# First token tile ahead of the second around the first expert gather: cross output, norm, queries and first list in another order

## The chip, the cores and the metric

The kernel runs on one core of one Trainium2 chip. The metric is the device time of one execution in microseconds; lower is better. The core has TensorE (PE, matmuls), VectorE (DVE), ScalarE (ACT), GpSimd (POOL) and SyncE (SP), which run their own instruction streams and meet at semaphores, and 16 DMA engines that move data for all of them.

## The reference

Batch 1, 256 tokens (two token tiles of 128), width 1024, float32. A first block (mLSTM, attention, gated feed-forward) is followed by a second block with two layers. Each layer has a mixer, a cross attention to 256 memory rows, and an expert layer that picks 128 of 16384 experts for each token (8 heads, 16 each):

```python
for l in range(2):
    h = h + mixer_l(rmsnorm(h, mix_norm[l]))
    h = h + memory_cross_attn(rmsnorm(h, xattn_norm[l]), mem_n, wq[l], wkv[l], wo[l])
    h = h + peer_ffn(rmsnorm(h, peer_norm[l]), peer_wq[l], peer_keys[l], peer_u[l], peer_v[l])

# peer_ffn, per token:
q = (xb @ wq).reshape(T, 8, 2, 128)
s = einsum('thpd,hpnd->thpn', q, sub_keys)                 # 2 x 128 scores per head
s1, i1 = top_k(s[:, :, 0], 16);  s2, i2 = top_k(s[:, :, 1], 16)
cand = s1[..., :, None] + s2[..., None, :]                 # 256 candidates per head
top, pos = top_k(cand, 16)                                 # and with pos the expert numbers eid
act = gelu(einsum('td,ted->te', xb, u[eid]))
y = einsum('te,ted->td', softmax(top) * act, v[eid])
```

## The kernel before

Everything is one program, written out by hand for each engine; the order of the instructions is the order of the code. Weights lie in HBM as tiles of 128 x 4096 float32 (2 MB), cut into four parts of 512 KB (0.524 MB). SP loads the parts in one fixed order (`tiles_in_order`, `weights_in_order`) into a ring of 6 parts (`W`, `RAW_RING`): a part is asked for when the part six places before it has been used. A tile can serve both token tiles; in `product` it does so part by part. In `one_tile` one token tile uses the whole weight tile, and its parts are given back only in the pass with `last` true.

PSUM has 8 banks. `Plan` deals them out in the order of `add`: each stage claims the next bank and waits until ScalarE or VectorE (its taker) has emptied the stage before it there.

The expert layer is four chains, (layer, token tile) = (0,0), (0,1), (1,0), (1,1), of 128 rows each. A row j is one gather by POOL (L789): for each of the 128 tokens the row of u and v of its j-th expert, 1.05 MB. Eight slots (`rows_a`, `rows_b`, `rows_c`) form a ring; slot n is refilled when TensorE has used row n-8 (`rows_done`). Two rows are a group: VectorE takes their dot products with the token (`dots`, L2511), ScalarE makes weights and two diagonal matrices of them (L1621 to L1632), TensorE adds v by them to the sum (`weigh`, L953, 4 matmuls of 512 columns in a group). `lead(c)` begins a chain and `feed()` does one group, and these calls are strewn among the other work of each engine, so that gathers run beside everything from the first one on. `drain()` does what is left of a chain.

The expert numbers come from VectorE in portions of two heads (32 rows): `top_lists` (the 16 best of 128 scores, four lists), `top_heads` (candidates, the 16 best of 256, twice), `top_keys` (from positions to expert numbers `p_eid`), `top_gates` (softmax over ScalarE's `top_exp`). The first portion stands ahead of the first row. The others are hung into the groups of chain 0 by the table `LISTS_AT[0]` (group: which chain and pair of heads), candidates 3 groups and key numbers 5 groups behind a list. POOL waits for `eid_ready` at every 32nd row.

The change lies in `joint`, the stage from the cross attention of layer 0 to the weights of layer 1's memory keys and values, where both token tiles are worked on together. In it stand, in this order on TensorE: query tiles `x_q`, scores `x_s`, transposes `x_t`, values `x_pv`, turned heads `x_oT`, output `x_o` (both weight tiles, token tile 0 then 1 for each), the turned normed tiles `T6.0` and `T6.1`, the expert queries and scores `p_q0` to `p_q3` and `p_s0` to `p_s3`, and the key and value tiles of layer 1, `x_k1` and `x_v1`, with the first groups of chain 0 among them.

## Time and profile before

| | us |
|---|---|
| median of 3 runs | 2315.01 |
| lowest, highest | 2313.47, 2315.64 |
| the profiled execution | 2322.3 |
| its span, first to last instruction | 2320.5 |

| engine | busy us | share of the span |
|---|---|---|
| PE | 2026.2 | 87% |
| DVE | 1498.7 | 65% |
| POOL | 926.9 | 40% |
| ACT | 766.8 | 33% |

777.34 MB are moved in all, 559.83 MB of them by POOL's queue, at a mean of 335 GB/s. The chain that ended last is 46% PE, 25% DMA and 21% DVE. A busy share is an average over stages with different limits; what a change in one stage is worth is read from the waits in that stage. Times in the trace count from the span's start. A float32 matmul leaves two records on PE, so x64 there stands for 32 matmuls.

### The profile page before, as it was taken

What the parts mean: (1) busy time and instruction counts of PE and PEld (TensorE: products, weight loads), DVE (VectorE), ACT (ScalarE), POOL (GpSimd) and SP (SyncE); (2) the same over time, 40 slices, a digit from 0 to 9 for tenths busy, and PEclk for the clock granted to TensorE, in tenths of its full rate; (3) what the DMA queues carried; (4) which work ended last, traced back from release to release, by engine and by line L of the source; (5) the groups of instructions that cost most, each with busy time, mean ns of one, the idle gap of its engine ahead of it and who ended that gap; (6) DMA issues with size and microseconds to landing.
All of it is one profiled execution on the core that took longest, in us unless ns stands there. A gap on an engine that the chain in (4) does not pass through costs nothing.

```text
span 2320.5 us, 25004 instructions
## 1 busy us (share of the span) xinstructions
PE 2026.2 (87%) x8348; PEld 1264.2 (54%) x8348; DVE 1498.7 (65%) x3776; ACT 766.8 (33%) x1771; POOL 926.9 (40%) x688
## 2 busy tenths in 40 slices
PE   8999999999999899997779988869999978777776
PEld 4855589878776455442345554624665536232322
DVE  5777523143324778886777776868786677877755
ACT  2323144444131333332333333233424222333332
POOL 2721368766421333443333233243323232444442
PEclk9999999999999999999999999999999989999999
DMA  8556455555324999999999999999999999999997
GB/s 321 213 192 211 173 182 191 196 199 198 138 100 159 423 423 422 419 391 420 423 420 398 391 419 420 418 421 385 423 379 389 377 420 369 399 416 425 413 425 298
DMA packets 139761, 777.34 MB, mean 335 GB/s; under 512 B 15512, under 2 KB 17688, under 8 KB 73072
## 3 DMA queue, kind: packets, MB, share of 16 engines
q0 software_dynamic: 79248, 559.83, 58.9%
q1 hardware_dynamic: 60240, 215.86, 25.0%
q8 instruction: 66, 1.08, 0.2%
q14 instruction: 63, 0.52, 0.1%
q10 hardware_dynamic: 144, 0.05, 0.0%
HBM read 774.62 MB, written 1.06 MB: 334 GB/s over the span
## 4 chain that ended last, share of the span: by engine, by line
PE 46%; DMA 25%; DVE 21%; ACT 4%; issue 2%; POOL 1%; SPq 0%; DVEq 0%; ACTq 0%; POOLq 0%
PE banks L953 14%; PE banks L842 14%; DMA rows_c<-in_uv,p_eid 12%; PE banks L990 7%; DMA W<-in_weights 6%; DMA rows_b<-in_uv,p_eid 5%; PE banks L1199 2%; DVE rows_b L2511 2%; DVE rows_c L2511 2%; DVE arena L2024 2%; DVE arena L2511 2%; DMA arena<-in_uv,p_eid 2%; PE banks L1429 2%; ACT arena L1623 1%; DVE arena L2280 1%
## 5 line engine op out<-in xcount | busy, mean ns | idle before, releaser
L953 PE MATMUL banks<-arena 128*128 128x512 f32 x712 | 348.1, 626 | 93.1 <-ACT arena L1632 92.8
L789 POOL DMA_INDIRECT arena<-in_uv,p_eid x192 | 219.3, 1142 | 495.3 <-PE banks L953 396.1
L724 POOL TENSOR_TENSOR W_lo<-W,W_hi 128x1024 fp32r<-128x1024 f32 x131 | 324.2, 2484 | 178.3 <-ACT W_hi L1570 127.6
L953 PE MATMUL banks<-rows_b,arena 128*128 128x512 f32 x668 | 322.8, 622 | 57.1 <-ACT arena L1632 57.1
L789 POOL DMA_INDIRECT rows_b<-in_uv,p_eid x192 | 213.3, 1111 | 301.3 <-PE banks L953 231.1
L1621 ACT ACTIVATE arena<-arena 128x2 f32<-128x2 f32 x256 | 52.0, 203 | 824.1 <-DVE arena L2030 823.3
L2511 DVE SCALAR_TENSOR_TENSOR arena<-arena,H 128x1024 f32<-128x1024 f32 x192 | 232.8, 1225 | 102.3 <-DMA arena<-in_uv,p_eid 99.5
L2511 DVE SCALAR_TENSOR_TENSOR rows_b<-rows_b,H 128x1024 f32<-128x1024 f32 x192 | 232.4, 1224 | 97.9 <-DMA rows_b<-in_uv,p_eid 96.1
L953 PEld LDWEIGHTS banks<-arena 128*128 128x128 f32 x712 | 133.3, 198 | 268.5 <-issue 137.2
L953 PE MATMUL banks<-rows_c,arena 128*128 128x512 f32 x460 | 222.3, 626 | 51.9 <-ACT arena L1632 51.9
L953 PEld LDWEIGHTS banks<-rows_b,arena 128*128 128x128 f32 x668 | 128.4, 198 | 229.2 <-issue 143.4
L1570 ACT ACTIVATE W_hi<-W 128x1024 fp32r<-128x1024 f32 x144 | 151.9, 1059 | 291.3 <-PE banks L842 172.4
L789 POOL DMA_INDIRECT rows_c<-in_uv,p_eid x128 | 148.0, 1156 | 250.4 <-PE banks L953 230.6
L1623 ACT ACTIVATE arena<-arena 128x1 f32<-128x1 f32 x512 | 198.0, 387 | 17.2
L2511 DVE SCALAR_TENSOR_TENSOR rows_c<-rows_c,H 128x1024 f32<-128x1024 f32 x128 | 154.6, 1224 | 74.1 <-DMA rows_c<-in_uv,p_eid 72.6
L842 PE MATMUL banks<-HT_hi,W_hi 128*128 128x256 f32 x640 | 183.2, 286 | 6.0 <-DVE W_lo L2444 4.7
L842 PE MATMUL banks<-HT_hi,W_lo 128*128 128x256 f32 x640 | 181.8, 284 | 0.0
L842 PE MATMUL banks<-HT_lo,W_hi 128*128 128x256 f32 x640 | 181.8, 284 | 0.0
L990 PEld LDWEIGHTS banks<-arena,W 128*128 128x128 f32 x1312 | 157.3, 196 | 34.3 <-issue 20.8
L990 PE MATMUL banks<-arena,W 128*128 128x128 f32 x1312 | 160.5, 280 | 16.8 <-DMA W<-in_weights 14.3
L953 PEld LDWEIGHTS banks<-rows_c,arena 128*128 128x128 f32 x460 | 87.4, 199 | 160.7 <-issue 87.7
L1632 ACT ACTIVATE arena<-const,arena 128x128 f32<-128x128 f32 x460 | 162.4, 395 | 8.3
(315 smaller groups left out, 3055.1 us busy)
## 6 DMA issues: line engine op xcount, KB each, us to landing
W<-in_weights SPq DMA_DIRECT2D x384, 512.0 KB, 6.7
sum_in<-in_sums POOLq DMA_DIRECT2D x24, 512.0 KB, 4.9
gain<-in_rows SPq DMA_DIRECT2D x7, 512.0 KB, 11.5
gain<-in_rows POOLq DMA_DIRECT2D x6, 512.0 KB, 5.1
arena<-in_keys SPq DMA_DIRECT2D x3, 1024.0 KB, 9.0
arena<-in_uv,p_eid POOLq DMA_INDIRECT x192, 11.7
rows_b<-in_uv,p_eid POOLq DMA_INDIRECT x192, 12.4
arena<-in_rows POOLq DMA_DIRECT2D x1, 2048.0 KB, 14.8
```

The costliest lines, as they stand in the source:

```text
L724: po.tensor_tensor(W_lo[:, slot, :], W[:, (PARTS * n + part) % RAW_RING, :], W_hi[:, slot, :].bitcast(F32), ALU.subtract).then_inc(S_("lo_ ...
L789: po.indirect_dma_start(rows[slot], None, io[f"uv{l}"], bass.IndirectOffsetOnAxis(ap=p_eid[:, t, j:j + 1], axis=0))\
L842: mm = pe.matmul(bank[:, out], x if stationary else y, y if stationary else x, start=start, stop=last)
L953: mm = pe.matmul(banks[:, plan.bank(f"p_v{c}", b), :], diag[:, m % DIAGS, :], rows[slot][:, D + b * BLK:D + (b + 1) * BLK], start=j == 0, ...
L990: mm = pe.matmul(bank[:, out], x if stationary else y, y if stationary else x, start=part + b + j == 0, stop=part == PARTS - 1 and b == le ...
L1199: mm = pe.matmul(banks[:, plan.bank("down", 2 * c + t), :], x[:, k, t * P:(t + 1) * P], w[:, c * BLK:(c + 1) * BLK], start=(i + part + m = ...
L1429: mm = pe.matmul(bank[:, out], x if stationary else y, y if stationary else x, start=part + b + j == 0, stop=part == PARTS - 1 and b == le ...
L1570: act.activation(W_hi[:, q % SPLIT_RING, :], wait_landed(act, n, part), ACT.Copy).then_inc(S_("hi_made"), 1)
L1621: step(act.activation(p_tanh[:, e], p_poly[:, e], ACT.Tanh, scale=0.7978845608028654))
L1623: step(act.activation(p_w[:, j:j + 1], p_tanh[:, j:j + 1], ACT.Identity, scale=p_half[:, j:j + 1], bias=p_half[:, j:j + 1]), "weight_ready ...
L1632: act.activation(diag[:, m % DIAGS, :], ident, ACT.Copy, scale=p_w[:, j:j + 1])\
L2511: v.scalar_tensor_tensor(out=u, in0=u, scalar=1.0, in1=H[:, t, :], op0=ALU.mult, op1=ALU.mult, accum_out=p_act[:, j:j + 1]).then_inc(S_("r ...
```

## The change

In `joint` the order and the weight loads change:

- PE turns and weighs token tile 0 through the cross attention first. Both halves of its output come next (`x_o.0`), then token tile 1's first half (`x_oa.1`), then the turned normed tile 0, its first queries and scores, then tile 1's second half (`x_ob.1`), then the first key tile of layer 1 (`x_k1`), and only then the turned normed tile 1 and `p_q1`. `p_q0.1` comes after the scores of `p_q1`.
- The two tiles of the cross output and the first query tile are loaded twice, since each pass now has its own. SP issues 396 parts, 384 before. The second key tile has the new name `x_k1b`.
- Chain 0 begins at part 2 of `p_q1`; groups also stand among the parts of `p_q1` and `p_q0.1`.
- VectorE does the first portion one head at a time. POOL may begin with 16 rows after `first_eid_ready`. The norm of token tile 1 comes after both heads.
- `LISTS_AT[0]` moves the other portions.

```diff
-LISTS_AT = [{2: (0, 1), 13: (0, 2), 20: (0, 3), 26: (1, 0), 33: (1, 1), 40: (1, 2), 48: (1, 3)}, {},
+LISTS_AT = [{7: (0, 1), 20: (0, 2), 27: (0, 3), 34: (1, 0), 40: (1, 1), 46: (1, 2), 52: (1, 3)}, {},
...
     p.add("x_q", 4, "scalar")
...
-    p.add("x_o", 4)
+    p.add("x_s.0", 2, "scalar")
+    p.add("x_s.1", 2, "scalar")
+    p.add("x_t.0", 2, "scalar")
+    p.add("x_pv.0", 2)
+    p.add("x_t.1", 2, "scalar")
+    p.add("x_oT.0", 2, "scalar")
+    p.add("x_pv.1", 2)
+    p.add("x_o.0", 2)
+    p.add("x_oT.1", 2, "scalar")
+    p.add("x_oa.1")
     p.add("T6.0", 2, "scalar")
     p.add("p_q0.0", taker="scalar")
+    p.add("p_s0.0", taker="scalar")
+    p.add("x_ob.1")
+    p.add("x_k1", 2, "scalar")
     p.add("T6.1", 2, "scalar")
...
-    t += [("x_q", 1), ("x_q", 3), ("x_o", 1), ("x_o", 3), ("p_q0.1", 0), ("p_q1", 1), ("p_q2", 1), ("p_q3", 1)]
-    t += [("x_k1", 1), ("x_k1", 3), ("x_v1", 1), ("x_v1", 3)]
+    t += [("x_q", 1), ("x_q", 3), ("x_o.0", 0), ("x_o.0", 1), ("x_oa.1", 0), ("p_q0.0", 0), ("x_ob.1", 0), ("x_k1", 1), ("p_q1", 1)]
+    t += [("p_q0.1", 0), ("p_q2", 1), ("p_q3", 1)]
+    t += [("x_k1b", 1), ("x_v1", 1), ("x_v1", 3)]
...
-                    if j % (2 * PK) == 0:
+                    if (c, j) == (0, 0):
+                        po.wait_ge(S_("first_eid_ready"), 1)
+                    elif j % (2 * PK) == 0 or (c, j) == (0, PK):
                         po.wait_ge(S_("eid_ready"), c * (PH // 2) + j // (2 * PK) + 1)
...
+                probabilities_turned(0)
+                values(0)
+                probabilities_turned(1)
+                heads_turned(0)
+                values(1)
                 after(pe, "x_oT.0", 1)
+                out("x_o.0", 0, 0)
+                out("x_o.0", 1, 0)
+                heads_turned(1)
                 after(pe, "x_oT.1", 1)
...
+                out("x_oa.1", 0, 1)
...
                 turned(0)
                 after(pe, "T6.0", 1)
...
-                turned(1)
+                queries_of("p_q0.0", "p_q0.0", 0, True)
                 pe.wait_ge(S_("keys_in"), 16)
                 scores(0, 0)
+                out("x_ob.1", 0, 1)
+                fills = [two_blocks("x_k1", j, 2 * P * j) for j in range(2)]
+                product(tile_no["x_k1"], fills, memT)
+                turned(1)
                 after(pe, "T6.1", 1)
...
-                scores(0, 1)
-                product(tile_no["p_q1"], [two_blocks("p_q1", j, 2 * P * j) for j in range(2)], j_HT)
+                fills = [two_blocks("p_q1", j, 2 * P * j) for j in range(2)]
+                for part in range(PARTS):
+                    if part == 2:
+                        lead(0)
+                    if part >= 2:
+                        feed()
+                    product(tile_no["p_q1"], fills, j_HT, part)
+                feed()
                 scores(1, 0)
                 scores(1, 1)
-                lead(0)
+                queries_of("p_q0.1", "p_q0.1", 1, True)
...
-                for i in range(3):
-                    add(i)
+                add("x_o.0", 0, 0, 0)
+                add("x_o.0", 1, 0, 1)
                 norm1(0, 6, 0)
-                add(3)
+                add("x_oa.1", 0, 1, 0)
+                top_lists(0, 0, (0,))
+                add("x_ob.1", 0, 1, 1)
+                top_heads(0, 0, p_work[0], (0,))
+                top_keys(0, 0, p_work[0], (0,))
+                top_lists(0, 0, (1,))
+                top_heads(0, 0, p_work[0], (1,))
+                top_keys(0, 0, p_work[0], (1,))
                 norm1(1, 6, 1)
-                top_lists(0, 0)
-                top_heads(0, 0, p_work[0])
-                top_keys(0, 0, p_work[0])
                 top_gates(0, 0)
                 lead(0)
```

`out` and `queries_of` call `one_tile` with `last` true. ScalarE's copies and `squares` follow in the same order (not shown), with `take_keys("x_k1", 0)` ahead of `top_exp(0, 0)`.

What that does to TensorE's stream, from the values of the cross attention to the first group of chain 0. Before (L1469 values, L1005 turning, L1429 `one_tile`: x_o with 512 columns, p_q0 with 128, L1487 scores p_s, L842 `product`, L953 groups):

```order
L1469 MATMUL banks<-arena 128x256 x16
L1005 MATMUL banks<-const,H 128x128 x16
L1429 MATMUL banks<-W,arena 128x512 x32
L1005 MATMUL banks<-const,H 128x128 x8
L1429 MATMUL banks<-arena,W 128x128 x32
L1005 MATMUL banks<-const,H 128x128 x8
L1487 MATMUL banks<-arena 128x128 x4
L1429 MATMUL banks<-arena,W 128x128 x32
L1487 MATMUL banks<-arena 128x128 x4
L842 MATMUL banks<-arena,W 128x256 x32
L1487 MATMUL banks<-arena 128x128 x8
L953 MATMUL banks<-arena 128x512 x6
```

And now, from tile 0's turned heads on (the same lines are L1018, L1487, L1444, L1523, L855 and L966 there):

```order
L1018 MATMUL banks<-const,H 128x128 x8
L1487 MATMUL banks<-arena 128x256 x8
L1444 MATMUL banks<-W,arena 128x512 x16
L1018 MATMUL banks<-const,H 128x128 x8
L1444 MATMUL banks<-W,arena 128x512 x8
L1018 MATMUL banks<-const,H 128x128 x8
L1444 MATMUL banks<-arena,W 128x128 x32
L1523 MATMUL banks<-arena 128x128 x4
L1444 MATMUL banks<-W,arena 128x512 x8
L855 MATMUL banks<-arena,W 128x256 x32
L1018 MATMUL banks<-const,H 128x128 x8
L855 MATMUL banks<-arena,W 128x256 x16
```

Three of the four x_o products now stand ahead of tile 0's queries and the fourth behind its scores. The x32 of L855 is the key tile x_k1; the x16 below it are the first two parts of p_q1, and chain 0's first group follows them.

VectorE's stream at the end of the first lists and the start of the candidates (`top_heads`, from p_cand on), before:

```order
L2763 CAST small<-p_idx 128x64
L2024 TENSOR_TENSOR p_cand<-small 128x512
L2747 MAX arena<-p_cand 128x8 x2
L2749 MAX_INDEX p_pos<-arena,p_cand 128x8 x2
L2751 MATCH_REPLACE arena<-arena,p_cand 128x256 x2
L2753 MAX arena<-arena 128x8 x2
L2755 MAX_INDEX p_pos<-arena 128x8 x2
```

And now:

```order
L2779 TENSOR_TENSOR X<-banks,X 128x512
L2803 MAX small<-arena 128x8 x2
L2805 MAX_INDEX p_idx<-small,arena 128x8 x2
L2807 MATCH_REPLACE arena<-small,arena 128x128 x2
L2809 MAX small<-arena 128x8 x2
L2811 MAX_INDEX p_idx<-small,arena 128x8 x2
L2820 CAST small<-p_idx 128x32
L2779 TENSOR_TENSOR X<-banks,X 128x512
L2075 TENSOR_TENSOR p_cand<-small 128x256
L2803 MAX arena<-p_cand 128x8
```

The adds of the cross output stood ahead of all lists. Now the fourth add (the second L2779) stands between the first head's list and its candidates, and each step is done for one head.

## Rows read from the trace of the kernel before

**Rows 1.** The page's 40 slices: DMA busy tenths and GB/s

```profile
DMA  8556455555324999999999999999999999999997
GB/s 321 213 192 211 173 182 191 196 199 198 138 100 159 423 423 422 419 391 420 423 420 398 391 419 420 418 421 385 423 379 389 377 420 369 399 416 425 413 425 298
```

**Rows 2.** Windows: stretch, length, busy us by engine (records), clock, DMA share, GB/s

```profile
680.00:690.00 10.00, 8.93 (x46) 7.58 (x47) 3.43 (x8) 3.34 (x8) 0.00 (x0) 1.00 0.00 0
746.00:748.00 2.00, 2.00 (x11) 1.77 (x10) 0.53 (x3) 0.00 (x0) 1.47 (x2) 1.00 0.18 43
748.00:750.00 2.00, 2.00 (x11) 1.77 (x10) 0.00 (x0) 0.00 (x0) 1.44 (x2) 1.00 0.88 287
...
758.00:760.00 2.00, 0.41 (x1) 0.44 (x2) 0.09 (x1) 1.64 (x5) 0.00 (x0) 0.79 1.02 424
760.00:762.00 2.00, 2.00 (x3) 0.73 (x3) 1.14 (x2) 0.00 (x0) 0.00 (x0) 0.50 1.03 432
762.00:764.00 2.00, 2.00 (x5) 0.90 (x4) 0.71 (x1) 0.00 (x0) 0.70 (x1) 0.86 1.02 422
764.00:1000.00 236.00, 220.82 (x649) 120.17 (x648) 195.64 (x647) 77.40 (x227) 91.87 (x83) 0.99 1.01 422
1000.00:1030.00 30.00, 29.12 (x69) 12.62 (x68) 26.51 (x80) 10.02 (x31) 14.03 (x12) 1.00 0.96 362
...
1130.00:2300.00 1170.00, 967.49 (x3600) 541.96 (x3599) 852.69 (x2230) 389.14 (x1075) 423.68 (x374) 0.95 0.99 407
```

**Rows 3.** Timeline, TensorE: start, us, engine line op, out<-in, shape, records, idle before

```profile
681.55 7.17 PE L1469 MATMUL banks<-arena 128*128 128x256 f32 x32 [0.60 <-ACT arena L1926]
...
691.85 27.70 PE L1429 MATMUL banks<-W,arena 128*128 128x512 f32 x64 [0.98 <-ACT arena L1666]
719.39 1.04 PE L1005 MATMUL banks<-const,H 128*128 128x128 f32 x8
721.37 7.41 PE L1429 MATMUL banks<-arena,W 128*128 128x128 f32 x64 [0.94 <-ACT arena L1666]
...
729.58 1.13 PE L1487 MATMUL banks<-arena 128*128 128x128 f32 x8
...
739.94 13.98 PE L842 MATMUL banks<-arena,W 128*128 128x256 f32 x64
...
759.59 5.15 PE L953 MATMUL banks<-arena 128*128 128x512 f32 x8 [2.87 <-ACT arena L1632]
...
1036.20 3.60 PE L842 MATMUL banks<-W,arena 128*128 128x512 f32 x8
```

**Rows 4.** Timeline, VectorE

```profile
712.80 0.69 DVE L2728 TENSOR_TENSOR X<-banks,X 128x512 f32<-128x512 f32 x1 [6.17 <-PE banks L1429]
...
717.19 1.28 DVE L2030 SCALAR_TENSOR_TENSOR H<-X,st,gain 128x1024 f32<-128x1024 f32 x1
...
731.50 0.88 DVE L2747 MAX8 small<-arena 128x8 f32<-128x128 f32 x4 [5.28 <-ACT arena L1666]
...
736.61 0.69 DVE L2024 TENSOR_TENSOR p_cand<-small 128x512 f32<-128x512 f32 x1
...
741.44 0.18 DVE L2785 TENSOR_SCALAR p_bits<-p_pos 128x32 uint32<-128x32 uint32 x1
...
745.76 0.19 DVE L2030 SCALAR_TENSOR_TENSOR p_eid<-p_i 128x32 uint32<-128x32 f32 x1
```

**Rows 5.** Timeline, POOL: gathers

```profile
746.23 1.01 POOL L789 DMA_INDIRECT arena<-in_uv,p_eid  x1 [81.23 <-DVE p_eid L2030]
...
763.30 0.94 POOL L789 DMA_INDIRECT arena<-in_uv,p_eid  x1 [6.98 <-PE banks L953]
...
1113.77 1.45 POOL L789 DMA_INDIRECT rows_b<-in_uv,p_eid  x1 [2.24 <-PE banks L953]
...
1118.70 1.37 POOL L789 DMA_INDIRECT rows_c<-in_uv,p_eid  x1 [2.24 <-PE banks L953]
```

**Rows 6.** DMA issues in 746 to 1130 us

```profile
W<-in_weights SPq DMA_DIRECT2D x27, 512.0 KB, 7.9
```

More of the change, by code:

```diff
@@ L236, in joint @@
             p.add(f"p_s{n}.{t}", taker="scalar")
-    p.add("x_k1", 4, "scalar")
+    p.add("x_k1b", 2, "scalar")
     p.add("x_v1", 4, "scalar")
@@ L328, in is_split @@
     return not (stage.startswith(("ada", "gate", "merge", "p_q")) or "." in stage or
-                stage in ("e_out", "x_o", "x_k1", "x_v1"))
+                stage in ("e_out", "x_o", "x_k1", "x_k1b", "x_v1"))
 def build(nc, io):
@@ L1369, in cross @@
                 after(pe, f"x_q.{c}", 1)
-                after(pe, "x_k1", 3)
+                after(pe, "x_k1b", 1)
                 for p in range(2):
@@ L1419, in queries, with one_tile @@
                     mm.then_inc(pe_filled, 1)
-            def one_tile(n, stage, i, blocks, last):
+            def one_tile(n, stage, i, blocks, last, between=None):
                 bank = claim(stage, i)
                 for part in range(PARTS):
+                    if between:
+                        between(part)
                     w = raw(n, part)
@@ L1460, in joint, with values @@
                         mm.then_inc(pe_filled, 1)
-                for t in range(NT):
+                def values(t):
                     after(pe, f"x_t.{t}", 1)
@@ L1515, in joint @@
                         feed()
-                        if n == 3 and part == 0:
-                            scores(2, 0)
-                            scores(2, 1)
+                        if part == 0:
+                            if n == 3:
+                                scores(2, 0)
+                            scores((0, 2)[n - 2], 1)
                         product(tile_no[f"p_q{n}"], fills, j_HT, part)
-                for n in range(2):
-                    fills = [two_blocks("x_k1", 2 * n + j, 2 * P * j) for j in range(2)]
-                    for part in range(PARTS):
-                        feed()
-                        feed()
-                        if n == 0 and part == 0:
-                            scores(3, 0)
-                            scores(3, 1)
-                        product(tile_no["x_k1"] + n, fills, memT, part)
+                fills = [two_blocks("x_k1b", j, 2 * P * j) for j in range(2)]
+                for part in range(PARTS):
+                    feed()
+                    feed()
+                    if part == 0:
+                        scores(3, 0)
+                        scores(3, 1)
+                    product(tile_no["x_k1b"], fills, memT, part)
                 for n in range(2):
@@ L1966, in joint @@
                 take_scores(3)
-                for n in range(2):
-                    feed(6 if n == 0 else 8)
-                    for j in range(2):
-                        take(x_kT[:, 4 * n + 2 * j:4 * n + 2 * j + 2, :], "x_k1", 2 * n + j)
+                feed(6)
+                take_keys("x_k1b", 1)
                 feed(16)
@@ new lines, in top_lists, with top_heads @@
+                top16([(p_v16[:, b0 + j, :], p_idx[:, j, :], src[:, j, :], work[:, j * NK:(j + 1) * NK]) for j in js])
+                step(v.tensor_copy(p_i16[:, b0 + js[0]:b0 + js[-1] + 1, :], p_idx[:, js[0]:js[-1] + 1, :]),
+                     "lists_ready" if 1 in heads else None)
+            def top_heads(c, n, work, heads=(0, 1)):
+                h0, those = 2 * n, slice(heads[0], heads[-1] + 1)
+                v16 = p_v16.rearrange("p (h a) k -> p h a k", a=2)[:, h0:h0 + 2][:, those]
+                shape = [P, len(heads), PK, PK]
+                tt(p_cand[:].rearrange("p (h a b) -> p h a b", a=PK, b=PK)[:, those], v16[:, :, 0, :].unsqueeze(3).to_broadcast(shape),
```

132 lines of the change are left out of this document (67 added, 65 removed).

## The prediction

> **What bounds the kernel now.** I read the page's slices first [rows 1]. The DMA share is 5 to 8 tenths while weights are streamed, falls to 2 in slice 12, and stands at 9 from slice 14 to the end. The windows [rows 2] give the edge: 0.18 in 746 to 748 us, 0.88 in the next 2 us, then 1.01 at 422 GB/s from 764 to 1000, and still 0.99 at 407 from 1130 to 2300. What switches it on is the first gather of expert rows, issued at 746.23 [rows 5]. From there to the end the kernel is, to a first approximation, a queue of bytes: 512 gathered rows of 1.05 MB and the weights that still have to come. TensorE is nearly as full (220.8 of 236 us in 764 to 1000), but two rows are asked for every 4.93 us where only rows are moved [rows 5], and that is 2.10 MB at 425 GB/s. So two things set the time: when the gathers start, and how many other bytes have to pass after that. Between 680 and 690 no byte moves at all [rows 2], since the weight ring is full and TensorE does cross attention. Bytes moved before 746 are therefore free as long as they come in time.
>
> The chain that leads to the first gather is read from the timelines of TensorE and VectorE. TensorE [rows 3]: values of the cross attention at 681.55 (7.17 us), cross output from 691.85 for 27.70 us, turning of the first normed tile at 719.39, its queries at 721.37, its scores at 729.58. VectorE [rows 4]: third add at 712.80, norm done at 718.47, lists of both heads from 731.50, candidates from 736.61, key numbers from 741.44, expert numbers done at 745.95. POOL issues at 746.23.
>
> **The change, step by step.** I carry the new chain forward with the durations of before.
>
> 1. Cross output. TensorE's work ahead of it is the same, in another order: tile 0's values need half of 7.17 us, and its turning no longer waits for tile 1. Before, two short waits stood here; I take 1.0 us off (bounds 0 and 1.2), so the products start at 690.9. Each of the four takes 27.70/4 = 6.9 us. Tile 0 has both halves at 704.7, not 712.7.
> 2. TensorE turns tile 1's heads and waits for the copies: 2.0 us, as from 719.39 to 721.37. Then comes the third product, to 713.5. Tile 0's norm took 5.7 us from the start of the add (712.80 to 718.47). From 704.7, and with those 2.0 us of ScalarE's copies ahead at worst, it is done by 712.4, hidden under the third product. Turning and copies take 2.0 us to 715.5, queries 7.4 us to 722.9, 0.8 us to the scores at 723.7, and 1.9 us more to the first list at 725.6 (before, 729.58 to 731.50). That is 5.9 us earlier than 731.50.
> 3. The list is done one head at a time. Both heads cost 5.1 us (lists), 4.8 us (candidates) and 4.5 us (key numbers). One head costs between half of that and all of it. Half of the elements or of the repetitions goes, the short fixed instructions stay, and with one job each instruction waits for the one before it. It is nearest to the half: I take 2.8, 3.1 and 3.0 us.
> 4. The add of the fourth product stands between the first head's list and its candidates. The list ends at 728.4, but the product starts behind the scores, at 724.8, and takes 6.9 us to 731.7. VectorE waits 3.3 us, adds, and goes on at 732.6. Candidates and key numbers end at 738.7, and the first gather is issued at 739.0. Term: 7.2 us earlier (bounds 4.3 with nothing halved, 8.6 with exact halves). Without that add it would be some 11 us.
> 5. Bytes. Two tiles of the cross output and one of the queries are loaded twice, 12 parts of 0.524 MB. Only those that pass after the first gather cost. Before, when the gathers start at 746.2, the first part of p_q1 is used (739.94 plus 13.98/4), the ring is 6 parts ahead, and 21 parts are left before layer 1: with the first 6 of that layer the 27 of [rows 6]. After, TensorE is two parts into the key tile x_k1 at 739.0 (it starts at 731.7, 3.5 us a part), so the ring ends with p_q1. Left are 4 parts of the reloaded p_q0.1, 8 of p_q2 and p_q3, 4 of x_k1b and 8 of x_v1, and the part just asked for: 25. Four parts more, at 0.524 MB and 424 GB/s 1.24 us each: 5.0 us later (bound below 3.7, if the last part has landed). The key tile moved ahead of the gathers has paid for one reload, not for all. The eight other parts pass before 739, where 24 parts in 55 us ask for 230 GB/s: nothing.
> 6. TensorE's hole. The second head's list takes 8.9 us (to 747.6), the norm of tile 1 follows (5.7 us less its add and its squares, some 3.8 us), to 751.4. TensorE finished the key tile at 745.5 and waits. Before, it waited 2.9 us ahead of 759.59, and the granted clock went to 0.79 and then 0.50 and came back in 762 to 764 [rows 2]: the first weighting took 5.15 us, where 8 such records take 27.70 x 8/64 = 3.46 us at full clock [rows 3]. The new hole is longer, so I charge the half clock in full: turning and copies 3 us, two parts of p_q1 7.0 plus 1.8 us, first row weighted from 763. Row 8 can be asked for at about 765 and flows at 767. Eight rows of 2.48 us and five parts of 1.24 us keep the queues full from 741 to 767. The two just meet: cost 1.0 us (bounds 0 and 3.5).
> 7. The other lists move from 2, 13, 20, 26, 33, 40, 48 to 7, 20, 27, 34, 40, 46, 52. The work is the same and VectorE has waits between. What they must not miss: rows 32 on need the second pair's numbers, ready after group 12's dots plus 4.5 us, when row 24 has just been weighted. I take nothing (bound 3 us). Masks, gains, layer 1 and the last chain keep their order.
>
> Sum: -7.2 + 5.0 + 1.0 = -1.2 us. The profiled execution took 2322.3 us (span 2320.5, 1.8 us around it), so the like of it would be 2321.1. The three timed runs lie 7.3 us lower at a median of 2315.01, and on them the same difference gives 2313.8.
>
> On the clock, the Trainium skill ("TensorE: Matmul & The Clock Gate", section Why this matters for your kernels) says that an idle stretch between bursts of matmuls puts the array back to half clock. By that rule both the hole of before and the longer new one cost clock; the trace agrees for the old one. Were the new hole to leave the clock alone, point 6 would be 0 and the sum -2.2 us. The rule speaks against the change, not for it.
>
> **Rivals.** (a) The likeliest is the sum above: 2313.8, own range 2310.5 to 2317.5, chance 0.42.
> (b) More gain. In 1000 to 1030 the DMA share is 0.96 at 362 GB/s [rows 2], which is 30 x (1 - 362/424) = 4.4 us of empty queue, at a place where VectorE was 26.5 of 30 us busy with lists of both tiles. If the new spacing closes it and the hole of point 6 is hidden, the sum is -7.2 + 5.0 - 4.4 = -6.6: 2308.4. For it speaks that lists come later, when only rows are moved. Against it: the spacing gets denser there (34, 40, 46, 52 against 33, 40, 48). Chance 0.27.
> (c) Slower. TensorE becomes the bound of this stage. It starts weighting at 763 and not at 759.6, with all 8 slots landed, so the ring is never ahead of it. From 759.59 until the end of the stage's last product (1036.20 plus 3.45) it had 280 us for 49 groups of two rows and 24 weight parts at 3.45 us each and some 6 us of scores, so about 20 us of waits. If they are no longer to be had, because each list on VectorE now holds up a TensorE that has no backlog of finished weights, the stage ends 3.4 us later plus the extra clock loss of 1.8 us: +5.2, 2320.2. It decides once the waits left fall under the 7.2 us that the queues run ahead. Against it: 10.3 us of TensorE for four rows and a part stand against 11.1 us of DMA, so it catches up 0.8 us a part. Chance 0.21.
> (d) The second pair's numbers come late for row 32 (point 7), and POOL stands for up to 3 us: +1.8, 2316.8. Chance 0.10.
>
> **The numbers.** 0.2% is 4.6 us, about what can be told from no change. Faster by more: (b) nearly whole and the edge of (a) and (d), 0.29. Slower by more: (c) and the edge of (d), 0.23. Within it: 0.48. The range over all cases, with the bounds of points 3 to 7, is 2306.5 to 2320.5.
>
> **What would show it.** First gather at 739, 7 us earlier; a wait of some 3 us on VectorE ahead of the fourth add; a half clock on TensorE between 748 and 757; DMA share 1.0 without a gap from 741, or a dent at 764 to 768 (point 6); 24 or 25 parts left; the end of the first 128 rows 1 to 3 us earlier. I am wrong if the gathers start before 736 or after 742, if the share dips again and again in 765 to 850 (then (c)), or if the stretch around 1000 to 1030 fills up (then (b)).

## The result, and the profile after

| | before | after |
|---|---|---|
| median of 10 runs, us | 2315.32 | 2324.56 |
| lowest, highest | 2312.43, 2321.04 | 2315.84, 2329.22 |
| the profiled execution | 2322.3 | 2327.81 |
| its span | 2320.5 | 2326.0 |

The ratio is 1.0031, 95% interval 1.0018 to 1.0043: 7.2 us slower (4.2 to 10.0). The two medians of the table lie 9.2 us apart; the ratio with its interval is what the text goes by. A second set of 12 runs, beside other kernels, gave 1.0022 (1.0009 to 1.0034). The forecast was 1.2 us faster, 2306.5 to 2320.5.

The profiles are read against a common mark, since executions already differ ahead of the changed stage: by 4.6 us in two profiles of the kernel before, by 4.9 in two of the changed one, by 16 over all 16 profiles of this document. The mark is the first score product of the cross attention, which all these kernels reach with the same work. TensorE's timeline of the kernel before, and below it of the kernel after:

```profile
670.82 7.17 PE L1449 MATMUL banks<-x_kT,arena 128*128 128x256 f32 x32 [0.75 <-ACT arena L1666]
```

```profile
672.56 7.17 PE L1464 MATMUL banks<-x_kT,arena 128*128 128x256 f32 x32 [0.75 <-ACT arena L1708]
...
683.29 3.72 PE L1487 MATMUL banks<-arena 128*128 128x256 f32 x16 [2.68 <-ACT arena L1968]
...
717.10 7.41 PE L1444 MATMUL banks<-arena,W 128*128 128x128 f32 x64 [0.94 <-ACT arena L1708]
...
753.07 1.97 PE L1018 MATMUL banks<-const,H 128*128 128x128 f32 x8 [5.95 <-DVE H L2081]
755.78 9.65 PE L855 MATMUL banks<-arena,W 128*128 128x256 f32 x32 [0.75 <-ACT arena L1708]
765.26 5.31 PE L966 MATMUL banks<-arena 128*128 128x512 f32 x12
```

So 1.74 us (672.56 less 670.82) of the profiled difference stood there before the change began; take it off every time of after. VectorE's and POOL's timelines of after:

```profile
727.23 0.49 DVE L2803 MAX8 small<-arena 128x8 f32<-128x128 f32 x2 [11.14 <-ACT arena L1708]
...
729.77 0.18 DVE L2820 CAST small<-p_idx 128x32 f32<-128x32 uint32 x1
733.41 0.69 DVE L2779 TENSOR_TENSOR X<-banks,X 128x512 f32<-128x512 f32 x1 [3.46 <-PE banks L1444]
...
740.08 0.17 DVE L2081 SCALAR_TENSOR_TENSOR p_eid<-p_i 128x16 uint32<-128x16 f32 x1
...
749.21 0.17 DVE L2081 SCALAR_TENSOR_TENSOR p_eid<-p_i 128x16 uint32<-128x16 f32 x1
```

```profile
740.54 1.01 POOL L802 DMA_INDIRECT arena<-in_uv,p_eid  x1 [73.79 <-DVE p_eid L2081]
...
767.42 0.94 POOL L802 DMA_INDIRECT arena<-in_uv,p_eid  x1 [16.68 <-PE banks L966]
```

From the mark the first gather comes after 67.98 us, 75.41 before: 7.4 us earlier, forecast 7.2. The one-head list takes 2.7 us, the wait for the fourth product is 3.46 us. All of the start happened as written. What was lost came later. The windows that show it are cut at gathers: first gather, row 8, 32, 64, 88, 112, 128, and the whole. Before (columns as in [rows 2]):

```profile
746.23:763.30 17.07, 13.45 (x58) 9.99 (x57) 4.44 (x12) 4.06 (x9) 7.95 (x9) 0.90 0.91 366
763.30:832.77 69.47, 63.88 (x195) 35.58 (x194) 49.09 (x149) 22.44 (x65) 25.60 (x25) 0.98 1.01 423
832.77:924.50 91.73, 87.20 (x274) 50.61 (x273) 79.89 (x274) 30.43 (x88) 37.12 (x33) 0.98 1.01 423
...
990.80:1059.58 68.78, 61.34 (x137) 25.93 (x136) 56.30 (x182) 22.68 (x66) 28.38 (x24) 0.98 0.99 392
1059.58:1104.39 44.81, 33.15 (x67) 13.15 (x66) 28.56 (x70) 13.37 (x40) 17.66 (x17) 0.92 1.02 425
746.23:1104.39 358.16, 321.75 (x891) 166.33 (x890) 277.02 (x880) 114.45 (x332) 144.13 (x129) 0.97 1.00 414
```

After:

```profile
740.54:767.42 26.88, 20.18 (x77) 15.96 (x76) 21.66 (x76) 7.63 (x20) 8.06 (x9) 0.81 0.95 377
767.42:839.01 71.59, 68.73 (x251) 41.53 (x250) 46.47 (x142) 21.96 (x62) 26.70 (x24) 0.95 1.00 409
839.01:930.54 91.53, 88.36 (x290) 52.75 (x289) 63.91 (x209) 31.41 (x89) 36.03 (x33) 0.98 1.01 417
...
996.72:1063.56 66.84, 58.59 (x129) 25.00 (x128) 63.69 (x220) 22.68 (x66) 29.45 (x25) 0.96 0.93 369
1063.56:1111.52 47.96, 34.14 (x67) 13.72 (x66) 35.22 (x94) 13.48 (x41) 16.35 (x17) 0.88 1.01 415
740.54:1111.52 370.98, 332.54 (x966) 178.68 (x965) 288.36 (x931) 116.97 (x337) 142.59 (x129) 0.95 0.99 405
```

Call "lost" the length times (1 - GB/s / 424), 424 being the rate that the full stretches show. GB/s is printed in whole numbers, which leaves 0.4 us open over the whole stretch. The whole was 358.2 us and is 371.0. Bytes: 358.16 x 0.414 = 148.3 MB before, 370.98 x 0.405 = 150.2 MB after, 2.0 MB or 4.6 us more. Lost: 8.4 us before, 16.6 after. The other 8 us are queues that ran empty or slow: 0.7 more in rows 0 to 8, 2.4 in rows 8 to 32, 1.3 in 32 to 64, 3.5 in 88 to 112, 1.1 in 112 to 128. With the start: -7.4 + 4.6 + 8.2 = +5.4 us at row 128, counted from the mark. (By the way in which "lost" is defined the parts must add up to this; what they tell is where the time went.) At the end of the span it is 3.8 us.

The weight parts issued from 738 to 1130 us of after, against 27 in [rows 6]:

```profile
W<-in_weights SPq DMA_DIRECT2D x31, 512.0 KB, 7.9
```

The page's slices of after, for [rows 1]; from slice 14 on they are again near full, with the dip at slice 18 deeper (359, before 391):

```profile
DMA  8656455555337999999999999999999999999997
GB/s 306 226 183 218 162 185 193 195 196 205 139 111 270 406 413 423 423 359 417 424 419 396 391 418 421 412 423 399 422 392 387 379 421 369 400 417 426 414 425 294
```

### The profile page after: what moved, and what is told of

It is laid out like the page before. It is cut to its first block, busy times and chain, and to the rows that moved or that the text cites. A ratio compares the mean times of both kernels' runs of the same rounds, so it can differ in the third digit from the quotient of the medians.

```text
span 2326.0 us, 25034 instructions
## 1 busy us (share of the span) xinstructions
PE 2031.4 (87%) x8348; PEld 1270.2 (55%) x8348; DVE 1501.1 (65%) x3789; ACT 766.5 (33%) x1771; POOL 928.9 (40%) x688
## 4 chain that ended last, share of the span: by engine, by line
PE 47%; DVE 23%; DMA 22%; ACT 4%; issue 2%; POOL 1%; SPq 0%; DVEq 0%; ACTq 0%; POOLq 0%
PE banks L855 15%; PE banks L966 15%; DMA rows_c<-in_uv,p_eid 10%; PE banks L1003 6%; DMA rows_b<-in_uv,p_eid 5%; DMA arena<-in_uv,p_eid 3%; DMA W<-in_weights 3%; PE banks L1212 2%; DVE rows_c L2562 2%; DVE rows_b L2562 2%; DVE arena L2075 2%; DVE arena L2562 2%; PE banks L1444 2%; ACT arena L1665 1%; DVE arena L2331 1%
## 5 line engine op out<-in xcount | busy, mean ns | idle before, releaser
L966 PE MATMUL banks<-arena 128*128 128x512 f32 x712 | 351.4, 634 | 98.7 <-ACT arena L1674 98.6
L966 PE MATMUL banks<-rows_b,arena 128*128 128x512 f32 x668 | 318.5, 614 | 47.4 <-ACT arena L1674 47.4
L966 PEld LDWEIGHTS banks<-arena 128*128 128x128 f32 x712 | 134.6, 199 | 273.4 <-issue 137.5
L966 PE MATMUL banks<-rows_c,arena 128*128 128x512 f32 x460 | 227.6, 639 | 52.7 <-ACT arena L1674 52.7
L966 PEld LDWEIGHTS banks<-rows_b,arena 128*128 128x128 f32 x668 | 128.3, 198 | 212.1 <-issue 141.5
L855 PE MATMUL banks<-HT_hi,W_hi 128*128 128x256 f32 x640 | 183.1, 286 | 5.1 <-DVE W_lo L2495 3.2
L855 PE MATMUL banks<-HT_lo,W_hi 128*128 128x256 f32 x640 | 182.2, 285 | 0.0
L855 PE MATMUL banks<-HT_hi,W_lo 128*128 128x256 f32 x640 | 182.2, 285 | 0.0
L966 PEld LDWEIGHTS banks<-rows_c,arena 128*128 128x128 f32 x460 | 89.2, 203 | 166.2 <-issue 91.3
L1003 PE MATMUL banks<-arena,W 128*128 128x128 f32 x1312 | 159.5, 280 | 15.5 <-DMA W<-in_weights 13.1
## 6 DMA issues: line engine op xcount, KB each, us to landing
rows_b<-in_uv,p_eid POOLq DMA_INDIRECT x192, 12.1
arena<-in_rows POOLq DMA_DIRECT2D x1, 2048.0 KB, 14.8
```

The costliest lines, as they stand in the source:

```text
L855: mm = pe.matmul(bank[:, out], x if stationary else y, y if stationary else x, start=start, stop=last)
L966: mm = pe.matmul(banks[:, plan.bank(f"p_v{c}", b), :], diag[:, m % DIAGS, :], rows[slot][:, D + b * BLK:D + (b + 1) * BLK], start=j == 0, ...
L1003: mm = pe.matmul(bank[:, out], x if stationary else y, y if stationary else x, start=part + b + j == 0, stop=part == PARTS - 1 and b == le ...
```

## The experiments

Three things stood to be separated: bytes, TensorE's late start, and the new table of places. Each kernel was timed against before, 5 rounds. "First" and "row 128" are counted from the mark and against the first profile of before (75.41 and 433.57 us); "lost" is of the stretch from the first gather to row 128; "end" is the span less the mark, against 1649.68 us of before. The mark itself stands in the second column. A profile is of one execution, and the two of the changed kernel differ by 3.0 us at row 128, so a smaller difference there is not shown by one profile.

| kernel | mark | ratio (95%) | first | row 128 | lost | end |
|---|---|---|---|---|---|---|
| before again | 666.24 | 1.0001 (0.9989, 1.0013) | 0.0 | 0.0 | 8.4 | +0.4 |
| changed | 672.56 | 1.0031 (1.0018, 1.0043) | -7.4 | +5.4 | 16.6 | +3.8 |
| changed again | 667.68 | 1.0022 (1.0009, 1.0034) | -7.4 | +2.4 | 14.8 | -1.4 |
| changed, spread places | 662.80 | 1.0004 (0.9988, 1.0020) | -5.8 | +2.5 | 12.1 | -1.4 |
| before, table alone | 661.00 | 1.0001 (0.9989, 1.0013) | 0.0 | +2.3 | 11.9 | +0.1 |
| changed, small parts | 664.60 | 1.0004 (0.9990, 1.0019) | -7.4 | +1.9 | 19.1 | -1.5 |
| changed, norm first | 666.11 | 1.0004 (0.9990, 1.0019) | -7.4 | +1.1 | 13.8 | -0.8 |
| changed, closer | 674.06 | 1.0000 (0.9988, 1.0013) | -7.4 | +2.0 | 13.0 | -4.6 |
| changed, spread, norm first | 670.52 | 1.0000 (0.9986, 1.0014) | -7.4 | -2.2 | 10.3 | -2.3 |
| changed, norm first, closer | 668.76 | 1.0000 (0.9989, 1.0011) | -7.4 | +0.5 | 13.0 | -3.8 |
| changed, norm first, small | 666.37 | 1.0001 (0.9986, 1.0015) | -7.4 | -1.3 | 15.5 | -4.6 |
| before, small parts | 677.22 | 1.0011 (0.9999, 1.0023) | 0.0 | -0.9 | 9.3 | -0.5 |
| before, heads | 666.43 | 0.9983 (0.9970, 0.9996) | -5.6 | -4.5 | 8.5 | -4.9 |
| before, heads, even places | 669.92 | 0.9992 (0.9978, 1.0006) | -5.6 | -4.7 | 8.5 | -5.9 |
| before, heads, closer | 667.63 | 0.9976 (0.9961, 0.9991) | -5.6 | -4.5 | 8.5 | -6.0 |

### The two controls

> The changed kernel once more, nothing edited, beside the other kernels of this call. Either theory: ratio to before 1.002 to 1.004 as measured first; counted from the first scores of the cross attention, first gather 7.4 us earlier and row 128 asked for 5 us later than before. If the ratio comes out at 1.000 to 1.001 instead, most of the 7 us measured first is not the change's.

> The kernel before, nothing edited, with a profile of its own in this call. All profiles since the first two show 8 to 12 us less between rows 176 and 184 than those two; either theory: here too, so this profile is the one to hold the others against; ratio 1.000.

The slowdown is real: 1.0022. The changed kernel's own profiles differ by 3.0 us at row 128, nearly all of it between rows 88 and 96. The first was one of its slower executions (2327.8 us, median 2324.6), the second one of its fastest (2317.8, median 2321.3), so neither end says as much as the ratios. The two profiles of before agree within 0.1 us at row 128. The second expectation was wrong: before shows the long stretch from row 176 to 184 again (last section).

### Places of the other portions

```diff
-LISTS_AT = [{7: (0, 1), 20: (0, 2), 27: (0, 3), 34: (1, 0), 40: (1, 1), 46: (1, 2), 52: (1, 3)}, {},
+LISTS_AT = [{7: (0, 1), 13: (1, 0), 20: (0, 2), 27: (0, 3), 34: (1, 1), 41: (1, 2), 48: (1, 3)}, {},
```

> The changed kernel with another table of places: pair (1,0) is done early, at group 13, and the six others at 7, 20, 27, 34, 41 and 48, so that no two portions follow each other by less than six groups and the last by seven (POOL's and ScalarE's counts follow the new order of the portions). Theory A (the places 40, 46, 52 let the key numbers of one portion and the lists of the next fall into successive groups, VectorE falls behind, TensorE waits and the queues run empty at 1000 to 1040 us): the 8.5 us that the DMA engines lose there fall back to the 4.3 us of the kernel before or less, row 128 is asked for about 4 us earlier, and the time is about 2320 to 2321, ratio to before 1.001 to 1.002. Rival B (the late start of the weighting alone makes TensorE the bound, whatever VectorE does): no difference from the changed kernel, ratio 1.003.

> The kernel before with nothing changed but the table of places (7, 20, 27, 34, 40, 46, 52). Theory A: slower than before by 3 to 4 us, with the loss at the same rows (88 to 110) and none in the first 100 us after the first gather; ratio 1.0013 to 1.0018. Rival B: within 1 us of before, since its weighting starts at 759.6 as ever.

The stretch of rows 88 to 112, in the spread kernel and in before with the new table alone:

```profile
989.16:1053.27 64.11, 57.71 (x129) 24.48 (x128) 55.09 (x187) 21.00 (x61) 25.45 (x25) 0.97 1.00 399
```

```profile
983.11:1049.91 66.80, 61.76 (x138) 26.01 (x137) 64.17 (x221) 22.67 (x66) 28.94 (x25) 0.97 0.96 377
```

Lost there: 3.8 us with the places spread (8.7 and 6.8 in the two profiles of the changed kernel), and the whole stretch to row 128 is 366.4 us long, 4.6 less than the 371.0 of the changed kernel, the 4 us of theory A, but only 1.6 less than the 368.0 of its second profile. Part of the 4.6 us is a later first gather (last section): row 128 comes 2.9 us earlier than in the first profile and no earlier than in the second. The ratio of 1.0004 is under the 1.001 to 1.002 expected. In before with the new table it is 7.4 (5.2 with its own). VectorE is busy 64 of 67 us in the kernels with the dense table, 55 of 64 in the spread one. So the table does cost by itself, 3.4 us of lost time and 2.3 us at row 128 (the two profiles of before agree within 0.1 there), at the rows that theory A names; in the time of before it did not show (1.0001), where 1.0013 to 1.0018 was expected and 1.0013 is the interval's edge. What happens on VectorE in the changed kernel, and on TensorE behind it:

```profile
985.43 0.18 DVE L2845 TENSOR_SCALAR p_bits<-p_pos 128x32 uint32<-128x32 uint32 x1
...
989.83 0.19 DVE L2081 SCALAR_TENSOR_TENSOR p_eid<-p_i 128x32 uint32<-128x32 f32 x1
...
992.93 0.87 DVE L2803 MAX8 small<-arena 128x8 f32<-128x128 f32 x4
...
997.80 0.20 DVE L2820 CAST small<-p_idx 128x64 f32<-128x64 uint32 x1
998.03 1.23 DVE L2562 SCALAR_TENSOR_TENSOR arena<-arena,H 128x1024 f32<-128x1024 f32 x1
```

```profile
1002.44 3.10 PE L966 MATMUL banks<-arena 128*128 128x512 f32 x4 [4.28 <-ACT arena L1674]
1005.33 2.51 PE L966 MATMUL banks<-rows_b,arena 128*128 128x512 f32 x4
```

With lists six groups apart, the key numbers of one portion (five groups behind their list) and the lists of the next fall into successive groups. Between 985.43 and 998.03 VectorE does one group of dot products and 9.6 us of portions. TensorE wants a group in 3.45 us, plus 3.45 for a weight part, uses up what it has, and waits 4.28 us. Then the slots come free late and the queues run dry. The group behind the wait takes 5.4 us (1002.44 to 1007.84) instead of 3.60.

### Successive steps, or load?

```diff
-HEADS_AT = [{g + 4: job for g, job in LISTS_AT[0].items()}, {},
+HEADS_AT = [{g + 3: job for g, job in LISTS_AT[0].items()}, {},
```

> The changed kernel with one number edited: candidates come 2 groups behind a list and key numbers 4, instead of 3 and 5. The lists stay at 7, 20, 27, 34, 40, 46, 52, so the load of VectorE is the same, but the key numbers of one portion and the lists of the next no longer fall into successive groups where the spacing is six. Theory A1 (it is the two in a row that open the 4.3 us hole on TensorE at 1002 us): the DMA engines lose 4 to 5 us in the like of 990 to 1050 us, not 8.9, and row 128 comes 4 us earlier than in the changed kernel. Rival A2 (it is the load: 15 us of lists and 17 us of dot products in six groups): the loss stays at 8 to 9 us.

```profile
996.56:1058.65 62.09, 56.66 (x130) 24.00 (x129) 59.72 (x203) 22.68 (x66) 27.68 (x24) 1.00 0.97 388
```

Lost in rows 88 to 112: 5.3 us, the 4 to 5 that A1 expected; in rows 8 to 32 it is 1.4, not 2.5 to 2.9. Row 128 is 3.4 us ahead of the first profile of the changed kernel, but only 0.4 ahead of the second. The ratio went from 1.0022 and 1.0031 to 1.0000. So the expectation of A1 was met at the rows that it names. But the loss partly moved forward, and the sum over rows 64 to 112 speaks against A1:

| | rows 64 to 88 | rows 88 to 112 | sum |
|---|---|---|---|
| before | 0.6 | 5.2 | 5.8 |
| before, table alone | 0.5 | 7.4 | 7.9 |
| changed, first and second profile | 0.3, 0.8 | 8.7, 6.8 | 9.0, 7.6 |
| changed, closer | 1.8 | 5.3 | 7.1 |
| changed, norm first | 0.6 | 8.1 | 8.7 |
| changed, norm first, closer | 3.2 | 5.5 | 8.7 |
| changed, spread places | 0.6 | 3.8 | 4.4 |

Closer candidates change where the queues lose, hardly how much; the table of places changes how much. And successive steps stood elsewhere without a loss: in before, the key numbers of the list at group 20 fall into group 25 and the next list into group 26, and rows 32 to 64 lose 0.2 us; in the changed kernel those of group 34 fall into 39 and the next list into 40, and rows 64 to 88 lose 0.3 us. That the table makes the loss is shown; that it does so by steps in successive groups, and not by the load of portions that stand closer there, is not.

### The norm of tile 1

```diff
+                norm1(1, 6, 1)
                 top_lists(0, 0, (1,))
                 top_heads(0, 0, p_work[0], (1,))
                 top_keys(0, 0, p_work[0], (1,))
-                norm1(1, 6, 1)
```

and on ScalarE:

```diff
                 take_keys("x_k1", 0)
+                take_tile("T6", 1)
                 top_exp(0, 0)
-                take_tile("T6", 1)
```

> The changed kernel with the norm of token tile 1 ahead of the second head's lists on VectorE, and ScalarE's copies of T6.1 ahead of its exponentials. TensorE then does not wait 6 us for the normed tile: T6.1 at about 748 instead of 753, p_q1 at full clock, first weighting at about 758.5 instead of 765. Theory B (the 3.9 us that the DMA engines lose in 760 to 860 come from this late start): they are won back, the time is about 2320.5, ratio 1.0022 less some. Rival (VectorE's lists cause those dips too): row 8 is asked for 6 us earlier but row 56 no earlier than 907, ratio 1.003.

```profile
742.67 7.17 PE L855 MATMUL banks<-arena,W 128*128 128x256 f32 x32 [1.13 <-ACT arena L1708]
751.64 3.67 PE L966 MATMUL banks<-arena 128*128 128x512 f32 x8 [1.79 <-ACT arena L1674]
```

The two parts of p_q1 take 7.17 us, not 9.65, and the weighting starts 85.5 us behind the mark, not 92.7. Lost in rows 8 to 64 falls from 4.0 to 1.3 us, row 8 comes 7.1 us earlier. Row 128 comes 4.3 us earlier than in the first profile of the changed kernel, 1.3 earlier than in the second. In rows 88 to 112 it still loses 8.1, 2.9 more than before: the norm's place does not touch the excess there. Theory B holds for rows 0 to 64; how much of it is left at row 128 (4.3 or 1.3 us) the two profiles of the changed kernel leave open.

### Bytes

```diff
+                cols = PW // 32 if tiles[n][0] in ('p_q0.1',) else PW
-                sp.dma_start(W[:, m % RAW_RING, :], io["weights"][weight_no[n]][:, part * PW:(part + 1) * PW])\
+                sp.dma_start(W[:, m % RAW_RING, 0:cols], io["weights"][weight_no[n]][:, part * PW:part * PW + cols])\
```

> The changed kernel, but of the four reloaded parts of p_q0.1 only one column in 32 is loaded (the queries of the second token tile's first pair are then made with what the ring held before; the work on every engine is the same). Bytes theory: the four parts passed while the queues were full, so the time falls by 4 x 1.24 = 5.0 us against the changed kernel, to about 2319.5, ratio 1.0018. Rival (TensorE bounds this stage, rows 0 to 50, and the bytes are hidden under it): 0 to 1 us, ratio 1.003.

> The kernel before, but of the four parts of p_q2, which pass right after the first gathers, only one column in 32 is loaded (its queries are then made with what the ring held before; the work on every engine is the same). Bytes theory: four parts less at a place where the queues are full all the time, 5.0 us less, ratio 0.998. Rival (something else, TensorE above all, would have set the pace a little later): 0 to 2 us, ratio 0.999 to 1.000, and the empty time of the queues before row 128 grows by what the bytes left.

> The changed kernel with the norm of token tile 1 ahead of the second head's lists, and one column in 32 of the four reloaded parts of p_q0.1 (its queries are then made with what the ring held before). With the parts small but TensorE late, only 0.5 to 3.5 us of the 5.0 came back by row 128 (two profiles of the changed kernel differ by 3), and 4 us of it turned up as empty queues right behind row 8. Bytes theory: now that TensorE is on time the whole 5 us comes back, row 128 is asked for some 3 to 4 us before its place in the kernel before (the norm alone: 1.1 us after it), and the time falls by 5 us against the norm alone, ratio 0.998. Rival (TensorE bounds rows 8 to 60 even then, and a transfer less is only an emptier queue): row 128 within 1.5 us of the norm alone, ratio 1.000.

Four full parts less pass behind the first gather (27, not 31), yet in the kernel with the late TensorE the lost time grows to 19.1 us. It comes in rows 0 to 32, where it is 9.2 us instead of 5.5: 3.7 of the 5.0 us turned into empty queues. With the norm first, row 24 is asked for 4.6 us earlier than with the norm alone, so the bytes do come back; but by row 64 the gain is down to 0.3 us:

```profile
826.14:920.63 94.49, 89.30 (x290) 53.02 (x289) 63.38 (x204) 30.84 (x87) 33.35 (x32) 0.96 0.99 401
```

That is 5.1 us lost there, 1.1 without the edit, and at row 128 the gain is 2.4 us. Neither expectation held: the four parts are worth 4.6 us for 24 rows, and about half of that at row 128. The times do not tell the kernel with norm first from the one with small parts besides (1.0004 and 1.0001). Small parts without the norm, at 1.0004, did fall by as much as the bytes theory asked for or more; but the edits that take no byte out fell as far, so this is no proof of it. The edit to before, with p_q2 in the list, was a poor one: when its first gather is issued the ring is 6 parts ahead, and only one of the four parts fell behind it (26 full ones, not 27). One part is 1.2 us, and row 128 came 0.9 us earlier. The time did not fall (1.0011).

### One part of the change alone

The functions of the changed kernel, and in `joint` of before:

```diff
-                top_lists(0, 0)
-                top_heads(0, 0, p_work[0])
-                top_keys(0, 0, p_work[0])
+                for h in range(2):
+                    top_lists(0, 0, (h,))
+                    top_heads(0, 0, p_work[0], (h,))
+                    top_keys(0, 0, p_work[0], (h,))
```

> The kernel before with one part of the change alone: the first portion head by head, POOL's first 16 rows behind the first head's numbers. Order on TensorE, the weight loads (384 parts) and the table stay. By the lengths in the trace of the changed kernel (2.7 us for one head's list, 6.1 us for its candidates and key numbers, against 14.4 us for both heads before) the first gather comes 5.5 us earlier, counted from the scores of the cross attention. Both heads together take some 3.5 us longer, so the weighting starts that much later, but eight rows and the weight parts among them last until row 8 can be asked for at about 763 to 767. Theory (bytes decide): row 128 is asked for 4 to 5 us earlier, ratio 0.998. Rival (TensorE's later start is kept to the end): row 128 2 to 3 us later, ratio 1.001.

```profile
736.27:1095.49 359.22, 324.74 (x917) 171.13 (x916) 285.10 (x918) 114.92 (x334) 142.94 (x128) 0.98 1.01 414
```

The first gather comes 5.6 us earlier, the stretch to row 128 is 359.2 us long and loses 8.5 us, as before, and the gain is kept: 4.5 us at row 128, 4.9 at the end, ratio 0.9983. The numbers expected for the bytes theory all held. Its TensorE is busy 3 us longer in the stretch than before, the changed kernel's 10.8 (332.54 against 321.75; 329.81 in its second profile).

### Repairs together

> The changed kernel with both repairs: pair (1,0) at group 13 and the rest at 20, 27, 34, 41, 48, and the norm of token tile 1 ahead of the second head's lists. If the two losses are separate and add up, row 128 is asked for 1 to 3 us earlier than in the kernel before (7.4 us of start, less 5.0 us of bytes, plus what is closed of the gap at 990 to 1050), ratio 0.999. Rival (one loss moves into the other): row 128 at the place of the kernel with one repair, 1 to 2.5 us later than before.

> The changed kernel with two edits: the norm of token tile 1 ahead of the second head's lists, and candidates 2, key numbers 4 groups behind a list. If the two losses are separate (about 3 us in the first 115 us after the first gather, about 3 us around rows 88 to 110), both are closed: from the first gather to row 128 the queues lose some 8 us instead of 13 to 14, row 128 is asked for 2 to 3 us earlier than before, ratio 0.999. Rival (the closer candidates only help because TensorE is late): no gain over the norm alone, ratio 1.0004.

> The kernel before with the first portion head by head, and the other portions at even distances of seven groups (2, 9, 16, 23, 30, 37, 44, the pair (1,0) second), candidates 2 and key numbers 4 groups behind a list. The head by head part alone gave 0.9983. If the queues' loss around rows 88 to 110 comes from portions too close together late in the stage, it falls from some 3 to 5 us to under 2, and the ratio is 0.997. Rival (the lists only move the loss to where weights are still streamed, as pair (1,0) at group 13 did to the changed kernel): 0.998 or worse.

> The kernel before with the first portion head by head, and candidates 2, key numbers 4 groups behind a list; its table of lists is untouched. Head by head alone gave 0.9983 and left 8.5 us of empty queues between the first gather and row 128, 5.3 of them in rows 64 to 112. Theory (two portions' steps in successive groups make those): they fall to 3 us or less, ratio 0.9975. Rival (it is VectorE's load there): unchanged, 0.998.

Spread places and norm first do add up at row 128: 10.3 us lost, 2.2 us earlier than before, as expected. In rows 64 to 112 they lose 6.1 us, where spread places alone lost 4.4; 3.4 of it is in rows 64 to 88. The time says 1.0000, no better than either repair; the reordered kernel, repaired, is even with before and not better. Norm and closer candidates together did not do as expected: they open a new loss of 3.2 us in rows 64 to 88 (0.6 with the norm alone) and stay at 13.0. With heads alone, even places only move the loss (0.9992). Closer candidates on top of heads:

```profile
986.80:1049.35 62.55, 59.47 (x138) 25.61 (x137) 56.66 (x175) 22.68 (x66) 29.42 (x25) 1.00 1.01 416
```

They bring rows 88 to 112 from 2.9 to 1.2 us, rows 64 to 88 from 2.4 to 3.8, the sum unchanged. So the expected fall to 3 us did not come. The ratio of 0.9976 is the best measured, 5.6 us under before (2.1 to 9.0); that it beats heads alone is not shown.

Four different single edits of the changed kernel (places, small parts, norm, closer) each gave a ratio between 1.0000 and 1.0004, and no pair of them went below 1.0000. Closer candidates, and spread places with norm first, were timed beside the changed kernel and lie 4 us under it in the median; for the other three the intervals overlap with that of the changed kernel. So the times do not say how the slowdown divides between the losses. That division is read from the rows of single profiles.

## Why the prediction was wrong, point by point

- **Points 1 to 4 held.** Less 1.74 us, the cross output starts at 690.7 (forecast 690.9), the first list at 725.5 (725.6), the first gather at 738.8 (739.0). VectorE's wait was 3.46 us (3.3).
- **Point 5, the bytes: count right** (31 parts, 25 and the 6 of layer 1). The 5.0 us is the right price only while the queues are the bound; taking the bytes out gave 2.4 us at row 128 with the norm first, and 3.5 or 0.5 without it, by which profile of the changed kernel one counts.
- **Point 6 failed in its price, not in its times.** The weighting started at 763.5 (763) and row 8 was asked for at 765.7 (765), with TensorE at 0.63 of its clock in between:

```profile
750.00:764.00 14.00, 10.19 (x35) 8.42 (x36) 10.65 (x30) 4.54 (x12) 0.74 (x1) 0.63 1.01 425
```

  I checked only that eight rows and five parts last until row 8. That was nearly so: rows 0 to 8 lost 3.0 us, 2.3 before. But TensorE, which is busy all 50 us from 770 to 820 (46.6 of them before), freed the slots late from then on. VectorE had to wait 46.7 us for rows between 770 and 900, 23.7 before, and with no finished weights in store a portion on VectorE opened a hole on TensorE (2.86 us at 826.29, below). Lost in rows 8 to 64: 3.7 us more than before (3.8 in the second profile), and 0.7 in rows 0 to 8, where 1.0 was charged in all. With the norm first, rows 8 to 64 lose 1.3 us: this is the late start.
- **Point 7 failed by as much.** "I take nothing (bound 3 us)" for the table; measured 4.6 us more lost in rows 88 to 128 (2.5 in the second profile), 3.4 over the stretch with the table alone in before. I looked at when the numbers are due, and not at what closer portions leave VectorE for dot products in rows 88 to 112: with the new table it is busy 64 of 67 us. In the first profile this step is the larger miss, in the second point 6 is.
- **Nearest to what happened is rival (c)**, given 0.21 at +5.2 us: the lists hold up a TensorE with no backlog. My argument against it, that TensorE catches up 0.8 us a part, left out those waits. TensorE was busy 10.8 us longer between the first gather and row 128 than before. Some 8 us of this is work (7.7 with the norm first): all of p_q1, T6.1 and p_q0.1 stand behind that gather now, and only about half a key tile stands ahead of it that stood behind. The rest is half clock, 2.5 us in the two parts of p_q1 alone (9.65 against 7.17 us). That (c) came near in size as well is partly luck: it had no term for the table.
- **Rival (b)** was wrong in its sign. The gap of [rows 2] at 1000 to 1030 did not close, it deepened (392 to 369 GB/s in rows 88 to 112). The reason noted against it, the denser spacing, is borne out: the table alone does it too (377).
- **Rival (d)** did not occur: POOL never waited for the second pair's numbers; its waits at row 32 end with TensorE.

The sum of what was measured is 5.4 us at row 128 and 3.8 us at the end of one profile, 2.4 and -1.4 in another, and 7.2 and 5.1 us by the ratios of the timed runs. How the rows behind 128 take up or give back a few us from run to run stays open; no experiment went there.

On the clock, behind a hole of 2.86 us TensorE weighted a group in 6.77 us, at a granted clock of 0.54, where 3.60 is its time at full clock:

```profile
826.29 6.77 PE L966 MATMUL banks<-rows_c,arena 128*128 128x512 f32 x8 [2.86 <-ACT arena L1674]
```

So a hole of 3 us cost 6. The Trainium skill ("TensorE: Matmul & The Clock Gate", section Why this matters for your kernels) says that idle stretches between bursts cost clock; the trace agrees here. It does not everywhere: in the second profile of the changed kernel a group behind a hole of 3.78 us took 3.70 us at a granted clock of 1.00:

```profile
1088.28 3.70 PE L966 MATMUL banks<-rows_b,arena 128*128 128x512 f32 x8 [3.78 <-ACT arena L1674]
```

## What to carry to other kernels

When an earlier start is bought by moving matmul work behind it, count the work that each engine has left in the stage as well as the bytes: an engine that starts with nothing in store can be stopped by a burst of another engine that it used to ride over. Where portions are hung into a loop, a table of places is a change of its own, even if every portion is still in time for its rows: add up what each stretch asks of the engine. Add up a loss over neighbouring stretches before you call it closed. And test the parts of a change apart: here the smallest one, head by head, was worth 4 us (0.9 to 7.0), and the reordering around it cost more than it brought.

## What was not expected of the hardware

Up to the first gather the profiles repeat: 67.97 or 67.98 us from the mark in eight of the nine profiles of kernels with the new order. In the ninth (spread places) it is 69.66, since the values of tile 0, which come behind a hole of 2.69 us, took longer, at a granted clock of 0.70 in 673.5 to 676 us:

```profile
673.53 5.41 PE L1488 MATMUL banks<-arena 128*128 128x256 f32 x16 [2.69 <-ACT arena L1969]
```

In each of the eight others the same 16 records take 3.72 us, behind a hole of 2.68 us. The same hole cost 0 eight times and 1.7 us once. Groups in the weighting show the same: behind holes of 2.49 us (norm first, at 818.02) and 3.78 us (above) they took 5.40 and 3.70 us.

```profile
818.02 5.40 PE L966 MATMUL banks<-rows_c,arena 128*128 128x512 f32 x8 [2.49 <-ACT arena L1674]
```

So what one such hole costs in one execution is uncertain by about 2 us.

Both profiles of before and the first of after wait in layer 1 for two weight parts, here before:

```profile
1276.71 2.58 PE L990 MATMUL banks<-arena,W 128*128 128x128 f32 x16 [3.08 <-DMA W<-in_weights]
...
1281.37 3.68 PE L990 MATMUL banks<-arena,W 128*128 128x128 f32 x16 [2.08 <-DMA W<-in_weights]
```

In the second profile of the changed kernel this wait is absent, and it goes from 1.8 us behind before at row 176 to 5.8 ahead of it at row 184; by row 320 it is 2.0 ahead. A marker inside a stage can therefore be off by more than the effect that one looks for, and only what repeats, or the medians, should carry a verdict.
